# RWKV's last doubling of a 128-row triangular inverse replaced by a substitution in two halves of 64 rows

## The reference, cut to what matters

```
def step(S, inp):
    r_t, w_t, k_t, v_t, kk_t, a_t = inp
    sa = einsum("bhvk,bhk->bhv", S, -kk_t)
    S = S * w_t + sa (kk_t * a_t)^T + v_t k_t^T
    return S, einsum("bhvk,bhk->bhv", S, r_t)
```

## Time and profile before

| | us |
|---|---|
| median of 3 runs | 3521.06 |
| lowest, highest | 3520.26, 3524.63 |
| the profiled execution | 3522.8 |
| its span, first to last instruction | 3520.7 |
| TensorE matmuls busy | 3264.9 |
| weight loads busy (beside matmuls) | 2679.9 |
| VectorE busy | 1278.6 |
| ScalarE busy | 678.5 |

### The profile page before, as it was taken

One profiled execution on the slowest core, in us unless ns is written; L12 is line 12 of the kernel. 1 busy time (PEld: TensorE's weight loads), 2 busy tenths in 40 slices (PEclk: granted clock), 3 DMA queues, 4 the chain that ended last, 5 costly groups with the idle time before them and its releaser, 6 DMA issues. The chain is left out here.

```text
span 3520.7 us, 37901 instructions
## 1 busy us (share of the span) xinstructions
PE 3264.9 (93%) x15948; PEld 2679.9 (76%) x15948; DVE 1278.6 (36%) x2763; ACT 678.5 (19%) x1261; POOL 60.7 (2%) x70
## 2 busy tenths in 40 slices
PE   7999998989999999899899999999999969997999
PEld 6888886878886888888787886885768548755784
DVE  3556656356321564756546321100310030016100
ACT  2223323123101332323122110100110020003000
POOL 0000000000000000000000000000000000000000
PEclk9999998999999999999999999999999989997999
DMA  4323222323333322232233324344334424421442
GB/s 187 109 82 117 86 93 89 104 81 116 110 129 132 121 81 101 97 104 99 69 104 108 114 86 180 126 153 146 130 108 150 140 78 151 148 98 72 138 150 107
DMA packets 153992, 404.46 MB, mean 115 GB/s; under 512 B 57536, under 2 KB 106816, under 8 KB 109920
## 3 DMA queue, kind: packets, MB, share of 16 engines
q1 hardware_dynamic: 51376, 367.87, 29.0%
q10 hardware_dynamic: 100608, 28.32, 3.3%
q0 software_dynamic: 1840, 5.84, 0.5%
HBM read 389.41 MB, written 12.59 MB: 114 GB/s over the span
## 5 line engine op out<-in xcount | busy, mean ns | idle before, releaser
L411 PE MATMUL bank<-h_features,weight_ring 128*128 128x256 f32 x7072 | 1589.3, 383 | 12.4 <-DVE h_features L494 4.9
L411 PEld LDWEIGHTS bank<-h_features,weight_ring 128*128 128x128 f32 x7072 | 1343.0, 192 | 201.4 <-issue 10.5
L1728 PE MATMUL bank<-weight_ring,ff_act 128*128 128x512 f32 x704 | 303.1, 592 | 4.6 <-DVE ff_act L1811 4.6
L1728 PEld LDWEIGHTS bank<-weight_ring,ff_act 128*128 128x128 f32 x704 | 133.4, 190 | 172.6 <-issue 166.5
L1811 DVE TENSOR_TENSOR ff_act<-ff_silu,bank 128x256 f32<-128x256 f32 x88 | 37.0, 421 | 577.2 <-ACT ff_silu L1802 577.2
L428 PE MATMUL bank<-weight_ring,h_features 128*128 128x256 f32 (+2 forms) x896 | 202.6, 377 | 1.9 <-DVE h_features L494 1.9
L428 PEld LDWEIGHTS bank<-weight_ring,h_features 128*128 128x128 f32 x896 | 163.2, 192 | 26.1 <-issue 3.3
L1802 ACT ACTIVATE ff_silu<-bank 128x256 f32<-128x256 f32 x88 | 33.7, 383 | 571.9 <-PE bank L411 571.9
L796 PE MATMUL bank<-rw_bm,rw_scored_a 128*128 128x64 f32 x768 | 105.0, 282 | 21.6 <-DMA rw_ex<-xT_scratch 21.6
L1665 PE MATMUL bank<-y_features,weight_ring 128*128 128x256 f32 x512 | 120.1, 387 | 0.0
L796 PEld LDWEIGHTS bank<-rw_bm,rw_scored_a 128*128 128x128 f32 x768 | 100.1, 200 | 25.6 <-issue 24.2
(11 more groups left out here) (428 smaller groups left out, 3596.7 us busy)
## 6 DMA issues: line engine op xcount, KB each, us to landing
weight_ring<-in_w_in SPq DMA_DIRECT2D x146, 1024.0 KB, 4.9
weight_ring<-in_f00w SPq DMA_DIRECT2D x33, 1024.0 KB, 4.8
weight_ring<-in_f01w SPq DMA_DIRECT2D x33, 1024.0 KB, 4.8
weight_ring<-in_f10w SPq DMA_DIRECT2D x33, 1024.0 KB, 4.8
weight_ring<-in_f11w SPq DMA_DIRECT2D x33, 1024.0 KB, 4.8
weight_ring<-in_w_b SPq DMA_DIRECT2D x16, 1024.0 KB, 4.8
weight_ring<-in_w_out SPq DMA_DIRECT2D x16, 1024.0 KB, 4.8
weight_ring<-in_conv_in SPq DMA_DIRECT2D x10, 1024.0 KB, 4.8
```

Of the source, the lines that this page charges most:

```text
L411: m = e.matmul(bank[:, j, :], w[:, k, j * P:(j + 1) * P], x[:, k, :], start=k == 0, stop=k == kt - 1, skip_group_check=True)
L1728: m = e.matmul(banks[i], src[:, k0 + k, t * P:(t + 1) * P], w[:, k, s * 512:(s + 1) * 512], start=k0 + k == 0, stop=k0 + k == k_tiles - 1, ...
```

## The change

`RW_LEVELS` loses 64, so the inverse stops at blocks of 64, two of them on the diagonal. The other half is a substitution, in the order of the direction: with `lo` the half of 64 rows that comes first and `hi` the other, w[lo] = inverse[lo] rhs[lo] (`w0`); rhs[hi] += A[lo to hi] w[lo] (`rest`); w[hi] = inverse[hi] rhs[hi] (`w1`). Each is four products of 64 rows by 64 columns with 64 moving columns, and a copy of 64 partitions by ScalarE stands behind each. `x` of level 32 isn't needed any more. `prod` and `xT` of a level share a bank, its first and second half, as do `rhs` and `w`. `rest` adds onto `rhs` in PSUM. Only the first product into the `rhs` bank opens it (start); the others write or add by the bank's own state. The reload of the inverse for step 1 waits for `w1`. The strings of `ORDER` for the mixers are new for TensorE, VectorE, ScalarE and SP.

```diff
-RW_LEVELS = (16, 32, 64)
+RW_LEVELS = (16, 32)
+def halves(d):
+    return (slice(0, 64), slice(64, 128)) if d == 0 else (slice(64, 128), slice(0, 64))
...
 (rwkv_pe: rhs)
-                        e.matmul(bank[:, n * P:(n + 1) * P], R.kr[:, n, c, 0, :], R.state[:, n, :], start=True,
+                        e.matmul(bank[:, n * P:(n + 1) * P], R.kr[:, n, c, 0, :], R.state[:, n, :], start=h == 0,
                                  stop=False, skip_group_check=True)
-                    m = e.matmul(bank[:, hs], R.scored_k[:, h, 0, :], R.vt[:, c, hs], start=step == 0, stop=True,
-                                 skip_group_check=True)
+                    m = e.matmul(bank[:, hs], R.scored_k[:, h, 0, :], R.vt[:, c, hs], start=step == 0 and h == 0,
+                                 stop=True, skip_group_check=True)
...
-                    if lv < 64:
+                    if lv == BLOCK:
                         bank = level_packed(g.banks.take(S, "x", *W, lv), lv)
...
-                    bank = level_packed(g.banks.take(S, "xT", *W, lv), lv)
-                    for free in g.banks.free("xT", *W, lv):
-                        e.wait_ge(*free)
-                    if lv == 64:
+                    bank = level_packed(g.banks.get("prod", *W, lv)[:, 2 * P:], lv)
+                    if lv > BLOCK:
                         e.wait_ge(*act.at("prod", *W, lv))
                         e.wait_ge(*dve.at("xT", *W, lv // 2))
...
-                bank = g.banks.take(S, "w", *W)
-                for free in g.banks.free("w", *W):
-                    e.wait_ge(*free)
-                e.wait_ge(*act.at("rhs", *W))
-                e.wait_ge(*dve.at("xT", *W, 64))
+                lo, hi = halves(d)
+                rest = g.banks.get("rhs", *W)
+                bank = rest[:, 2 * P:]
+                e.wait_ge(*act.at("rhs", *W, 0))
+                e.wait_ge(*dve.at("xT", *W, 32))
                 for h in range(4):
                     hs = slice(h * 64, h * 64 + 64)
-                    m = e.matmul(bank[:, hs], R.xT[:, h, :], R.rhs[:, hs], start=True, stop=True, skip_group_check=True)
-                m.then_inc(*pe.up("w", *W))
+                    m = e.matmul(bank[lo, hs], R.xT[lo, h, lo], R.rhs[lo, hs], start=False, stop=True,
+                                 skip_group_check=True)
+                m.then_inc(*pe.up("w", *W, 0))
+                yield
+                e.wait_ge(*act.at("w", *W, 0))
+                for h in range(4):
+                    hs = slice(h * 64, h * 64 + 64)
+                    m = e.matmul(rest[hi, hs], R.scored_a[lo, c, h, 0, hi], R.w[lo, hs], start=False, stop=True,
+                                 skip_group_check=True)
+                m.then_inc(*pe.up("rest", *W))
+                yield
+                e.wait_ge(*act.at("rhs", *W, 1))
+                for h in range(4):
+                    hs = slice(h * 64, h * 64 + 64)
+                    m = e.matmul(bank[hi, hs], R.xT[hi, h, hi], R.rhs[hi, hs], start=False, stop=True,
+                                 skip_group_check=True)
+                m.then_inc(*pe.up("w", *W, 1))
                 yield
...
-                e.wait_ge(*act.at("w", *W))
+                e.wait_ge(*act.at("w", *W, 1))
...
 (rwkv_act)
-                    e.wait_ge(*pe.at("w", l, q, d, 0))
+                    e.wait_ge(*pe.at("w", l, q, d, 0, 1))
...
-                e.copy(R.rhs, g.banks.get("rhs", *W)[:, 0:2 * P]).then_inc(*act.up("rhs", *W))
-                g.banks.empty(act, "rhs", *W)
+                e.copy(R.rhs[lo, :], g.banks.get("rhs", *W)[lo, 0:2 * P]).then_inc(*act.up("rhs", *W, 0))
...
-                    g.banks.empty(act, "prod", *W, lv)
...
-                e.wait_ge(*pe.at("w", *W))
-                e.copy(R.w, g.banks.get("w", *W)[:, 0:2 * P]).then_inc(*act.up("w", *W))
-                g.banks.empty(act, "w", *W)
+                e.wait_ge(*pe.at("w", *W, 0))
+                e.copy(R.w[lo, :], g.banks.get("rhs", *W)[lo, 2 * P:]).then_inc(*act.up("w", *W, 0))
+                yield
+                e.wait_ge(*pe.at("rest", *W))
+                e.copy(R.rhs[hi, :], g.banks.get("rhs", *W)[hi, 0:2 * P]).then_inc(*act.up("rhs", *W, 1))
+                yield
+                e.wait_ge(*pe.at("w", *W, 1))
+                e.copy(R.w[hi, :], g.banks.get("rhs", *W)[hi, 2 * P:]).then_inc(*act.up("w", *W, 1))
+                g.banks.empty(act, "rhs", *W)
...
```

13 lines of the change are left out of this document (6 added, 7 removed), and 94 rows, old and new, of the table ORDER.

## The result

| | before | after | difference |
|---|---|---|---|
| median of the runs shown with it, us | 3520.66 (3517.47 to 3524.63, 4 runs) | 3470.89 (3465.36 to 3475.62, 4 runs) | -49.8 |
| ratio, 95% interval | | 0.9858 [0.9842, 0.9874] | |
| profiled execution, span | 3520.7 | 3463.6 | -57.1 |

The kernel became 1.4% faster. The forecast was 3486 us with a range of 3450 to 3530: direction and range held, and the median lies 15 us under the forecast.

What follows compares the result with a forecast made beforehand. TensorE's order in the two mixer stages was taken as the bound. From 3522.8 us, 37 less work (71 out, 34 for switches) and 2 more waits gave 3487.8 profiled, 3486 by the median; range 3450 to 3530.

Steps and rivals of the forecast that it cites:

- parts 1 and 2: TensorE work in 32 units: 71 us taken out, 34 us added by tile switches, together 37 us less.
- Rival (a): New 64x64 groups: small tiles bring no shorter step, 0.111 us an instruction stays; +8, 3529 us; chance 0.13.
- rival (c): New small groups: the switches are hidden, or idle time falls further; 3452 us by the median; chance 0.17.
- rival (d): New groups: half products run as full-array ones, no switch, no shorter step; 3495 us; chance 0.06.
- part 3: Waits in the mixer stages under the new order: +1 us a layer, +2 in all.
- tail: Last quarter: `bonus` and `finish` lose their filler, norm's chain stands bare; net +10 us a layer.
- end of quarter 2: Between `o` and `finR`: 12.2 us of pieces instead of 4.4, against the norm's 9.2; -14 us a layer.
- quarter 3: Ahead of `prod16`: 1.0 and 1.7 us less filler; +2.7 us a layer.
- quarter 2, direction 1: No filler from `w1` to the second right-hand side; +5 us a layer.
- quarter 2, direction 0: From the last `scored_a` to `prod16`: filler 18.2 us instead of 7.0; -11 us a layer.
- quarter 1, direction 0: Filler falls from 22.6 to 17.4 us, +5; bare chain end, slow clock, early retention finish; +8 us a layer.
- Rival (b): Gains in quarter 2 are taken back while tail and bare links cost as worked out; +15, 3536 us; chance 0.12.

Runs made afterwards that it cites:

- the four meetings: Kernel before, with four weight loads held back on SP until the reload of the inverse of their unit has landed: 3494.2 us, ratio 0.9935.
- the old order with the copy in time: Changed kernel in the order of before, with ScalarE copying `rest` right behind its copy of `w0`: 3503.8 us, ratio 0.9947; repeated 0.9967.
- split groups: Changed kernel with head 1's product in 160 `prod`, `x` and `xT` groups made as two 64-column halves: 3526.3 us, ratio 1.0023.

## Why the prediction was right, and where it was not

**Work, parts 1 and 2: right within 4 us.** Forecast -71 + 34 = -37 us, measured -41.3, or -40.5 as the mean of seven traces; some 2 us of the switches may count as idle time instead. The small step is 0.058 us against 0.056 taken, the switch pair 0.34 (0.80 less 8 x 0.058) against 0.35, the `x` group 0.90 (28.9 us for 32 of them) against 0.89. The pair's split was wrong, and its sum right by luck: I had 0.15 us on entering and 0.2 on leaving, read from 64-row products of 128 columns, and a sign of it behind the groups; the trace has 0.30 on entering and 0.04 on leaving, and the idle load queue stands ahead of them. Rival (a), no shorter step, falls with the step of 0.058; rival (c), hidden switches, with the 0.80 us of a group; rival (d) with the 64*64 forms, and its price (+9 against my forecast) came out at 12 to 16.

**Bank sharing at nothing: right** (0.9984).

**The waits, part 3: this step failed.** Forecast +1 us a layer, measured -7 (idle -9.4 and clock -4.6 for both layers). By place, each the change of idle plus clock between two `o` groups (the end of quarter 2 reaches from its last `o` to 5 us behind `finish`, the tail from the last `o` but one to the end of the stage), layer 1 / layer 2; the last column is what a repeat of before moves:

| place | forecast | measured | repeat |
|---|---|---|---|
| tail | +10 | +8.4 / +8.0 | -1.6 / -0.2 |
| end of quarter 2 | -14 | -13.2 / -12.9 | -0.1 / 0.0 |
| quarter 3 | +2.7 | +5.0 / +5.4 | -4.8 / 0.0 |
| quarter 2, direction 1 | +5 | +7.2 / +4.9 | +0.1 / 0.0 |
| quarter 2, direction 0 | -11 | -5.0 / -4.9 | 0.0 / +0.1 |
| quarter 1, direction 0 | +8 | +1.9 / -1.6 | -3.8 / -0.3 |
| quarter 1, direction 1 | not listed | -8.0 / -7.7 | 0.0 / +0.2 |
| quarter 0 | not listed | -2.0 / +0.6 | +2.0 / +2.9 |

Four places were right within 3 us. In quarter 3 that is in part luck: ahead of `prod16`, for which the forecast had +2.7, TensorE waits 7.5 us more in each layer, and other waits there fell. Quarter 2, direction 0 gained less than half of what I gave it: I counted 11 us more filler as 11 us less waiting, but the waits moved to other products of retention, HGRN and RWKV (timeline of PE, after, against the earlier trace rows):

```profile
556.10 3.65 PE L1570 MATMUL bank<-rt_vt,rt_gam 128*128 128x256 f32 x8 [2.38 <-issue]
...
564.24 2.05 PE L1306 MATMUL bank<-hg_qs,hg_ks 128*128 128x128 f32 x8 [4.48 <-DVE hg_ks L1480]
...
569.96 3.65 PE L750 MATMUL bank<-rw_kr,rw_a 64*128 64x256 f32 x16 [3.68 <-DVE rw_a L1104]
```

Quarter 1 is what failed, by 6 to 10 us a layer in direction 0 and by 8 in direction 1. In direction 0 I held the arrival of the inverse fixed and counted TensorE's filler alone; the orders of ScalarE and VectorE move the arrival itself, here the issue of the reload by 10.7 us and its landing by 8.2. In direction 1 I did not look, since the filler hardly changes there; the wait was one of two transfers meeting, and the new order parts them. Both are one mistake: a wait has two ends, and I worked out only one. The total came within 15 us in part by luck: quarter 2, direction 0 took away 6 us a layer less than forecast and quarter 1 took away 14 to 17 more.

**Rival (b), bare ends**, had its mechanism at the tail and not its balance: the tail cost what it said, and the end of quarter 2 was not taken back.

**The signs.** "Idle time near 70 us each" came out at 60 and 65 in the tighter stages, where before has 65 and 70. The counts, the 64*64 forms, loads of 135 ns and the missing 7 us stall at the end of quarter 2 came as named; the bare stretch ahead of the last `finish` is 8.6 us from the last `o` to the transposes, with `bonus` in it, where 9 or more were named.

What stays open: how the order's 31 to 38 us divide between the meetings and the rest. For the old arithmetic the four meetings are worth 23 us. For the new arithmetic in the old order the kernel that was to show it did not hold its loads, and it was not tried again. Its traces say where to look: of the 35 us of idle time between the old order with the copy in time and the changed kernel, the waits ahead of `prod` make only 1 in sum (29.0 and 27.9 us). The largest parts are the waits ahead of the right-hand side and `o` (36.7 and 16.1), the gating mixer's products (30.3 and 18.7), retention's (12.2 and 3.3) and `w0` (13.0 and 4.5). Nor was TensorE's new order tried apart from that of the other engines. What sets the share of low clock from run to run isn't shown either: a repeat moves it by as much as the change did.

## What to carry to other kernels

Work priced by the step on the load queue came out within 4 us of 37; where the schedule stayed fixed, a third to more than a half of it went back into waiting and clock, and all of it where one step of a new chain had no place of its own on a helper engine. For a wait on data that goes through memory, work out both ends: when the consumer gets there, and when the transfer is issued and what else is in flight within 2 us of it; holding four large prefetches behind a small urgent reload gave 23 us for four waits. Before filling a hole, measure the hole behind it too: one piece moved from one to the other gave some 3 us (7 by the trace of the tail), enough filler for both gave 15 to 18.

## What the runs showed of the hardware

- A 256 KB reload, by all 14 traces, mostly lands in 3.1 to 3.7 us when no weight load is issued from 3 us ahead of it to its own issue (5.1 at the worst), in 3.9 to 5.3 with a 1 MB weight load issued 2 to 3 us ahead, in 5.2 to 6.6 with one issued between 2 us ahead and 0.2 behind, and in 8.0 to 8.7 with one on either side (once 6.0). Two cases lie outside: 9.3 with two issued 0.4 and 2.2 us behind it, and 8.2 with one issued at the same time and one 2.7 us ahead. That the weight load is the cause is shown for four directions, where it was held back.
- Lost time costs clock as well. Holding four loads back took away 15 to 17 us of idle and 17 to 34 us of low clock; one late copy in each unit had brought 11 to 16 and 20 to 44 (the lower and upper figures are two traces of the same kernel). Even 160 switch pairs that show as no more idle time of TensorE brought 61 us more at 1.2 GHz, half of their cost.
- In the split groups the four loads of 64 columns start in pairs, 7 ns apart within a pair and 48 from one pair to the next, where loads of the 64x64 groups start 58 ns apart. The trace doesn't say which loads make a pair; that they are of the two column halves, loaded at the same time, is my guess. The pair of switches around them costs 0.147 us on entering and 0.091 on leaving beyond the normal step of 0.112.
- The page "TensorE: Matmul & The Clock Gate" of the Trainium skill, Part 3, says under what overlaps that a load overlaps running matmuls only where the row groups differ; its mechanism section allows it for a load into the background weight buffer too. The 64x64 groups go with the second, as the full ones did: loads and matmuls of the same rows go at 0.058 us together, while either alone is an estimated 0.053 or 0.054.
